# A two-layer hybrid backbone: first layer's down projection in two token passes, value products by column halves, branch weights ahead of logits

## What is computed

```python
h = modulate(rms_norm(x, norm1[l]), shift, scale)      # latent and context have their own vectors
z = h @ w_in[l]                                        # projections of four branches, gate logits
ys = [retention(z), gated_linear(z), grouped_attention(z), differential_attention(z)]   # each (T, 256)
m = sum(sigmoid(gate[i]) * (ys[i] @ w_branch[l, i]) for i in range(4))
x = x + g1 * (m @ w_out[l])
u = modulate(rms_norm(x, norm2[l]), shift2, scale2) @ w_up[l]
x = x + g2 * ((silu(depthwise_conv(u[..., :2816])) * u[..., 2816:]) @ w_down[l])
```

## Time and profile before

| what | us |
|---|---|
| median of 3 runs | 3206.71 |
| the profiled execution | 3203.14 |
| its span, first to last instruction | 3201.3 |
| TensorE matmuls busy | 2903.1 |
| GpSimd busy | 1420.2 |
| VectorE busy | 1322.9 |
| ScalarE busy | 597.4 |

### The profile page before, as it was taken

One profiled execution on the slowest core, in us unless ns is written; L12 is line 12 of the kernel. 1 busy time (PEld: TensorE's weight loads), 2 busy tenths in 40 slices (PEclk: granted clock), 3 DMA queues, 4 the chain that ended last, 5 costly groups with the idle time before them and its releaser, 6 DMA issues.

```text
span 3201.3 us, 38109 instructions
## 1 busy us (share of the span) xinstructions
PE 2903.1 (91%) x15848; PEld 2364.0 (74%) x15848; DVE 1322.9 (41%) x1730; ACT 597.4 (19%) x958; POOL 1420.2 (44%) x1357
## 2 busy tenths in 40 slices
PE   7899988989989788999999996997889896789999
PEld 7689977777868666888885655785667675668877
DVE  0622126643356754555551017315653576232231
ACT  1210032212124421100110003003211144011110
POOL 1233417722322353556540004453933333768886
PEclk6789979999989888999999997998999898899999
DMA  7331311221220451343442122221222104523322
GB/s 238 87 87 61 99 46 57 60 60 47 68 58 27 125 181 33 106 119 107 118 119 79 50 69 83 76 63 38 72 53 60 40 31 132 151 67 98 99 82 83
DMA packets 375480, 266.31 MB, mean 83 GB/s; under 512 B 9691, under 2 KB 348287, under 8 KB 374796
## 3 DMA queue, kind: packets, MB, share of 16 engines
q1 hardware_dynamic: 372928, 261.03, 27.8%
q10 hardware_dynamic: 1612, 2.75, 0.2%
q0 software_dynamic: 768, 0.09, 0.0%
HBM read 234.48 MB, written 29.36 MB: 82 GB/s over the span
## 4 chain that ended last, share of the span: by engine, by line
PE 79%; DVE 11%; POOL 4%; ACT 2%; DMA 2%; issue 1%; SPq 0%; DVEq 0%; ACTq 0%; POOLq 0%
PE ps L413 15%; PE ps L414 14%; PE ps L415 14%; PE ps L868 7%; PE ps L539 4%; PE ps L466 4%; PE ps L589 3%; PE ps L451 2%; PE ps L452 2%; PE ps L453 2%; PE ps L607 1%; PE ps L511 1%; POOL w_lo L991 1%; DMA ring<-in_w_branch 1%; DVE arena L1364 1%
## 5 line engine op out<-in xcount | busy, mean ns | idle before, releaser
L988 POOL TENSOR_TENSOR w_hi<-ring,tiny 128x512 fp32r<-128x512 f32 x524 | 582.2, 1111 | 1614.2 <-PE ps L415 744.6
L413 PE MATMUL ps<-hh,w_hi 128*128 128x512 f32 (+1 forms) x2272 | 844.8, 372 | 50.7 <-DVE hl L1355 50.7
L414 PE MATMUL ps<-hl,w_hi 128*128 128x512 f32 (+1 forms) x2272 | 818.9, 360 | 0.0
L415 PE MATMUL ps<-hh,w_lo 128*128 128x512 f32 (+1 forms) x2272 | 817.1, 360 | 0.0
L991 POOL TENSOR_TENSOR w_lo<-ring,w_hi 128x512 fp32r<-128x512 f32 x524 | 719.2, 1373 | 41.1
L413 PEld LDWEIGHTS ps<-hh,w_hi 128*128 128x128 f32 x2272 | 440.9, 194 | 157.9 <-issue 59.5
L415 PEld LDWEIGHTS ps<-hh,w_lo 128*128 128x128 f32 x2272 | 440.3, 194 | 64.6
L414 PEld LDWEIGHTS ps<-hl,w_hi 128*128 128x128 f32 x2272 | 442.0, 195 | 57.7 <-issue 1.0
L868 PE MATMUL ps<-arena,ring 128*128 128x512 f32 (+1 forms) x704 | 230.1, 490 | 1.2 <-DVE arena L1718 1.2
L868 PEld LDWEIGHTS ps<-arena,ring 128*128 128x128 f32 x704 | 134.6, 191 | 96.2 <-issue 85.8
L1648 DVE SCALAR_TENSOR_TENSOR xT<-ps,modv,xT 128x512 f32<-128x512 f32 (+1 forms) x48 | 30.3, 659 | 392.6 <-PE ps L868 197.6
(11 more groups left out here) (206 smaller groups left out, 3891.8 us busy)
## 6 DMA issues: line engine op xcount, KB each, us to landing
ring<-in_w_in SPq DMA_DIRECT2D x118, 512.0 KB, 4.1
ring<-in_w_mod SPq DMA_DIRECT2D x96, 512.0 KB, 3.9
ring<-in_w_up SPq DMA_DIRECT2D x88, 512.0 KB, 4.0
ring<-in_w_down SPq DMA_DIRECT2D x32, 512.0 KB, 4.1
logits<-arena SPq DMA_DIRECT2D x32, 384.0 KB, 2.4
arena<-logits SPq DMA_DIRECT2D x32, 384.0 KB, 3.4
ring<-in_w_branch SPq DMA_DIRECT2D x16, 512.0 KB, 4.9
ring<-in_w_out SPq DMA_DIRECT2D x16, 512.0 KB, 4.4
```

Of the source, the lines that this page charges most:

```text
L413: pe.matmul(acc, wh[:, k], hi[:, n, x:y], start=n == 0, stop=False)
L414: pe.matmul(acc, wh[:, k], lo[:, n, x:y], start=False, stop=False)
L415: mm = pe.matmul(acc, wl[:, k], hi[:, n, x:y], start=False, stop=n == whole - 1)
L988: pool.tensor_tensor(wh[:, 0:count], w, one[:].unsqueeze(2).to_broadcast([P, count, P]), ALU.mult).then_inc(*up("w_lead", ("lead", key, j)))
```

## The change

**First layer's down projection.** It is done in two passes over tokens. The latent pass (chunks `down`) is split as in the second layer, with `ffh` and `ffl` made in both layers. The context pass (new chunks `dctx`, the same weights loaded a second time, not split) multiplies plain fp32 over 256 columns. Accumulators are one bank per output tile, `u % 4`. VectorE adds to the residual per stream (`residual_of`) and squares at once; TensorE sums the squares per stream (`sum_of_squares`), the latent ones between the output tiles and in the context pass, and the next layer's norm 1 runs per stream (`norm_of`): the latent one beside the context pass. The first two projections of the second layer (queries, latent only) wait for the latent norm alone; the third waits for the context part. The store to `x_kept` in the second layer moves from the first to the fourth projection's chunk.

**Value products.** Two heads are multiplied together in all branches but gla: the values (128 keys x 64) are the stationary operand and the turned weights (128 keys x 128 queries) move; the first head's result goes to partitions 0 to 63, the second's to 64 to 127 of `("oT", l, b, t)`. ScalarE (ret, dif) or VectorE (gqa) copies it to `o_turned`, and two transposes (`turn_back`) bring it to the former layout. In the softmax branches the products of a pair stand behind the transposes of the head after it, and the turning back of tile t - 1 in head 1 of tile t. The last tile of ret and gqa is turned back behind the next branch's first projection.

**Order.** SP issues branch weights two chunks ahead of the logits of an output tile (`AHEAD`); the last logits are stored with the third `wb` chunk. One gate tile moves from dif to behind dif, and there it comes before `turn_outputs`.

```diff
-AMONG = {0: dict(ret=8, gla=10, gqa=7, dif=7), 1: dict(ret=8, gla=10, gqa=7, dif=7)}
+AMONG = {0: dict(ret=8, gla=10, gqa=7, dif=6), 1: dict(ret=8, gla=10, gqa=7, dif=6)}
...
+        order += [("dctx", l, n // 3, n % 3) for n in range(3 * KT) if W[l] > LAT]
...
-    return key[0] not in ("mod", "slice") and not (key[0] == "down" and W[key[1]] > LAT)
+    return key[0] not in ("mod", "slice", "dctx")
...
+        squares_of = {"lat": lambda k: sqb[1][:, k % 2, 0:LAT], "ctx": lambda k: arena[:, (8 + k) * T:(8 + k) * T + CTX]}
+        span_of = {"lat": (0, LAT), "ctx": (LAT, T)}
...
+        o_turned = prep_flat[:, 0:512].rearrange("p (b c t) -> p b c t", b=2, c=2)
...
+            def sum_of_squares(part, k):
+
+                key, (x, y) = ("norm", 1, part), span_of[part]
+                if k == 0:
+                    for s, n in room(key, 4 if part == "lat" else 5):
+                        pe.wait_ge(s, n)
+                pe.wait_ge(*at(("sq", 1, part, k)))
+                pe.matmul(psum(key)[:, 0:y - x], K["ones"], squares_of[part](k), start=k == 0, stop=k == KT - 1).then_inc(
+                    *up("pe_squares", ("squ", 1, part, k), *([("full", key)] if k == KT - 1 else [])))
...
-            def value_product(l, b, t, h, weights, *also):
-                pt = weights[:, h % 2].rearrange("p (m n) -> p m n", n=P)
-                hv = h // 2 if b == "gqa" else h
+            def value_products(l, b, t, first, weights, *also):
+
+                pt = [weights[:, s].rearrange("p (m n) -> p m n", n=P) for s in range(2)]
+                c = first // 2
                 for m in key_tiles(t):
-                    mm = pe.matmul(psum(("o", l, b, t))[:, 64 * h:64 * h + 64], pt[:, m],
-                                   v[:, hv // 2, m, 64 * (hv % 2):64 * (hv % 2) + 64], start=m == key_tiles(t)[0], stop=m == NT - 1)
-                mm.then_inc(*up("pe_values", ("pv", l, b, t, h), *([("full", ("o", l, b, t))] if h == 3 else []), *also))
+                    for s in range(2):
+                        vt = v[:, 0, m, 64 * c:64 * c + 64] if b == "gqa" else v[:, c, m, 64 * s:64 * s + 64]
+                        mm = pe.matmul(psum(("oT", l, b, t))[64 * s:64 * s + 64, P * c:P * c + P], vt, pt[s][:, m],
+                                       start=m == key_tiles(t)[0], stop=m == NT - 1)
+                mm.then_inc(*up("pe_values", ("pv", l, b, t, first), ("pv", l, b, t, first + 1),
+                                *([("full", ("oT", l, b, t))] if c else []), *also))
+
+            def turn_back(l, b, t, *also):
+
+                pe.wait_ge(*at(("free", ("oT", l, b, t))))
+                acc = psum(("o", l, b, t))
+                for c in range(2):
+                    mm = pe.transpose(acc[:, c * P:(c + 1) * P], o_turned[:, t % 2, c], ident)
+                mm.then_inc(*up("pe_values", ("full", ("o", l, b, t)), *also))
+
+            def last_turn_back(l, b):
+                t = NQ[l] - 1
+                for s, n in room(("o", l, b, t), 5):
+                    pe.wait_ge(s, n)
+                turn_back(l, b, t)
 
             def retention(l):
                 b = "ret"
...
@@ retention, TensorE @@
-                        value_product(l, b, t, h, pt_r)
+                    value_products(l, b, t, first, pt_r)
+                    if first == 0 and t > 0:
+                        for s, c in room(("o", l, b, t - 1), 5):
+                            pe.wait_ge(s, c)
...
@@ softmax, TensorE @@
-                    turn_weights(t, h, n >= 1)
-                    if n >= 1:
-                        base[("o", l, b, order[n - 1][0])] = 5 * 512 + 256
-                        value_product(l, b, *order[n - 1], pt_s, ("full", ("pt", l, b, t, h)))
+                    base[("oT", l, b, t)] = base[("o", l, b, t)] = 5 * 512 + 256
+                    if h % 2 == 0 and n > 0:
+                        turn_weights(t, h, True)
+                        value_products(l, b, *order[n - 2], pt_s, ("full", ("pt", l, b, t, h)))
+                    elif h == 1 and t > 0:
+                        turn_weights(t, h, True)
+                        turn_back(l, b, t - 1, ("full", ("pt", l, b, t, h)))
+                    else:
+                        turn_weights(t, h, False)
                 t, h = order[-1]
                 pe.wait_ge(*at(("free", ("pt", l, b, t, h))))
-                value_product(l, b, t, h, pt_s)
-                tenant[5] = ("o", l, b, t)
+                value_products(l, b, t, h - 1, pt_s)
...
@@ main loop, TensorE @@
+                            each = None
+                            if b == "ret" and j == 0:
+                                each = lambda k: ("hl", l, 1 if l == 0 else "lat", k)
+                            if b == "ret" and j == BR[b]["nq"] and l > 0:
+                                each = lambda k: ("hl", l, "ctx", k)
+                            projection(("f", l, b, j), hh, hl, W[l] if is_q(b, j) else T, banks(), each=each)
                             behind(("f", l, b, j))
...
+                        if j == 0 and BEFORE.get(b) in ("ret", "gqa"):
+                            last_turn_back(l, BEFORE[b])
...
+                last_turn_back(l, "dif")
+                among(l, "after", 0)
                 turn_outputs(l, "dif")
-                among(l, "after", 0)
...
-                    for s, n in room(acc_key, 2 * (u % 3), 2 * (u % 3) + 1):
+                    for s, n in room(acc_key, u % 4):
...
-                        if is_split(key):
+                        for j in range(2):
+                            pe.wait_ge(*at(("split", key, j)))
+                            mm = product(acc[:, 0:LAT], key, j, ffh, ffl, 0, LAT, count=min(4, count - 4 * j),
+                                         first=8 * c + 4 * j, whole=FT, each=(lambda k: ("ffl", l, k)) if u == 0 else None)
+                            mm.then_inc(*up("pe_half", ("half", key, j), *([("full", acc_key)] if 2 * c + j == 5 else [])))
+                    if l + 1 < DEPTH and u >= 2:
+                        sum_of_squares("lat", u - 2)
+                if l + 1 < DEPTH:
+                    for u in range(KT):
+                        acc_key = ("dctx", l, u)
+                        for s, n in room(acc_key, u % 4):
+                            pe.wait_ge(s, n)
+                        for c in range(3):
+                            key = ("dctx", l, u, c)
+                            next_chunk(key)
...
+                            for k in range(8 * c, min(8 * c + 8, FT)):
+                                mm = pe.matmul(psum(acc_key)[:, 0:CTX], raw(key)[:, k - 8 * c], ff[:, k, LAT:T],
+                                               start=k == 0, stop=k == FT - 1)
                             mm.then_inc(*up("pe_raw", ("used", key), *([("full", acc_key)] if c == 2 else [])))
+                        if u == 0:
+                            sum_of_squares("lat", KT - 2)
+                            sum_of_squares("lat", KT - 1)
+                    for k in range(KT):
+                        sum_of_squares("ctx", k)
...
@@ SP @@
+            AHEAD = 2
...
-                if n >= LATE and chunks[n - LATE][0] == "g" and key[0] != "wb":
+                if n >= LATE and chunks[n - LATE][0] == "g" and not (key[0] == "wb" and key[2] > AHEAD):
                     store_logits(chunks[n - LATE])
-                if key == ("wb", l, 0):
-                    for late in chunks[n - LATE:n]:
+                if key == ("wb", l, AHEAD):
+                    for late in chunks[n - LATE + 1:n - AHEAD]:
                         store_logits(late)
-                if key == ("mod", 0, MOD0 - 1) or key == ("f", 1, "ret", 0):
+                if key == ("mod", 0, MOD0 - 1) or key == ("f", 1, "ret", 3):
                     for k in range(KT):
-                        sp.wait_ge(*at(("free", ("x", k)) if l == 0 else ("free", ("down", 0, k))))
...
-                if key[0] == "wb":
-                    u = key[2]
+                if chunks[n - AHEAD][0] == "wb":
+                    u = chunks[n - AHEAD][2]
...
@@ ScalarE @@
+            def norm_of(part):
+
+                key, (x, y) = ("norm", 1, part), span_of[part]
+                act.wait_ge(*at(("full", key)))
+                act.activation(rs[:, x:y], psum(key)[:, 0:y - x], ACT.Sqrt, bias=eps).then_inc(*up("act_free", ("free", key)))
+                for k in range(KT):
+                    act.wait_ge(*at(("scaled", 1, part, k)))
+                    act.activation(hh[:, k, x:y], tb[:, k % 2, x:y], ACT.Identity,
+                                   bias=modv[:, k, int(x > 0):int(x > 0) + 1]).then_inc(*up("lead_ready", ("hh", 1, part, k)))
...
+            def outputs_out(l, b, t):
+
+                key = ("oT", l, b, t)
+                act.wait_ge(*at(("full", key)))
+                if t >= 2:
+                    act.wait_ge(*at(("full", ("o", l, b, t - 2))))
```

(50 more changed lines are left out.)

80 lines of the change are left out of this document (42 added, 38 removed).

## The result

| | median us | lowest to highest | runs | ratio to before, 95% interval |
|---|---|---|---|---|
| before, same chip | 3205.85 | | 4 | 1 |
| the change | 3104.11 | 3097.84 to 3112.55 | 4 | 0.9683 [0.9653, 0.9714] |
| predicted | 3109 | 3072 to 3166 | | |

A forecast was written before the change was run, and what follows sets the result against it. TensorE was taken to bound the kernel, busy 2903.1 of 3201.3 us. Steps of -28, -43, -18 and -8 sum to -97, so 3203.1 becomes 3106, and 3.6 for the median gives 3109 us; range 3072 to 3166.

The forecast's parts named there:

- B: Value products of two heads in column halves, turned back afterwards: -43 us, bounds -52 and +12.
- C: Branch merging, weights loaded ahead of logits: -18 us, bounds 0 and -28.
- A: First layer's down projection in two passes, with the norm behind it per stream: -28 us, bounds -38 and -12.
- D: One gate tile moved behind the last branch, filling TensorE's wait there: -8 us, bounds 0 to -14.
- The idle before the second tile: Latent down pass: TensorE idles 9.4 us, the second tile's first weights queued behind a modulation slice awaiting its ring slot.
- the row halves: Attention scores with neighbours in different row halves, 24 records in 1.53 us, taken as nearest price for value products.
- without overlap: Rival on value products: column halves don't work side by side, so no gain there; 3163 us, chance 0.19.
- swallowed: Rival: engines beside TensorE take the value products' gain in the attentions, only retention keeps it; 3142 us, chance 0.13.
- unhidden loads: Rival on value products: column halves undo hiding of weight loads, 0.228 us a record; 3307 us, chance 0.06.
- the stall behind the restored stream: Layer 0's merging: logits wait behind the 3 MB residual load; 6 us of the 12 us stall stay.
- crowding loads: Branch merging: loads at 206 GB/s, above the stage's 193, get in each other's way; 5 us back.

The follow-up runs named there:

- e6: The changed kernel with the last four modulation slices of the weights loaded three down chunks later; 3099.5 us, ratio 0.9679 to before.
- e4: The changed kernel with the moved gate tile put back inside differential attention and none behind it; 3111.03 us, ratio 0.9704 to before.
- e5: The changed kernel with all value products of a group's first head before the second's, so neighbours share a column half; 3146.56 us, ratio 0.9822 to before.
- e2: The changed kernel with value products as before, one head at a time and no turning back; 3148.1 us, ratio 0.9817 to before.

## Why the prediction was right, step by step

**Sum.** Predicted -97 on the profiled execution, measured -97.0; 3109 against 3104.11 us. The mechanisms are the ones that were named, but the match to the last microsecond is luck. The edited stages give 92 us, and 5.4 of those are the granted clock of one stretch; the rest comes from stages where the two kernels do the same. The repeated change is 95.9 us of medians under before, the first 101.7. Inside B and C errors cancel, as shown below. One sum doesn't come out: the bounds given for A, C and D reach from 3083 to 3151, not from 3080 to 3138.

**A, -28 predicted; -25.3 in the trace, 26 by undoing.** The idle before the second tile was to be 9.4 us and is 10.66, by the mechanism named, which e6 confirms. The latent pass was to end 154 us after zero and ends at 154.4. (The 113.76 us that the prediction quotes from the earlier trace rows stand in the earlier trace rows.) The context pass was to end at 239 and ends at 235.6 (1866.0): its sums start at once, and no last residual stands between. But the chain behind it was mis-sized, and it is why A gives 25 and not 28. I gave 13 us from there to the strips, a third of the joint norm, and had the strips at 252; they begin at 256.9, 21.3 us behind the context's sums. (My zero before, 1677.65, was the first down product; from the end of the up projection, 1676.4, the old strips stand at 281.7, so they came 24.8 us nearer.) VectorE and GpSimd in order of time:

```profile
1877.07 1.26 DVE L1433 SCALAR_TENSOR_TENSOR hl<-arena,modv,hh 128x256 fp32r<-128x256 f32 x1
1878.36 1.36 DVE L1440 SCALAR_TENSOR_TENSOR arena<-xT,tiny,arena 128x256 f32<-128x256 f32 x1
1879.65 0.47 DVE L1433 SCALAR_TENSOR_TENSOR hl<-arena,modv,hh 128x256 fp32r<-128x256 f32 x1
1880.16 0.48 DVE L1440 SCALAR_TENSOR_TENSOR arena<-xT,tiny,arena 128x256 f32<-128x256 f32 x1
...
1887.34 1.09 DVE L1542 SCALAR_TENSOR_TENSOR arena<-dist,arena 128x896 f32<-128x896 f32 x1 [3.53 <-ACT arena L1274]
```

```profile
1878.12 1.32 POOL L1054 TENSOR_TENSOR w_lo<-ring,w_hi 128x512 fp32r<-128x512 f32 x1
1889.46 1.04 POOL L1051 TENSOR_TENSOR w_hi<-ring,tiny 128x512 fp32r<-128x512 f32 x1 [10.02 <-PE ps L420]
```

Over 256 columns a scaling (L1440) takes 1.36 to 1.40 us and a rest (L1433) 1.26 while GpSimd splits weights, and either takes 0.48 from 1879.65 on, after GpSimd's last split ended. The eight tiles take 14 us, where a third of the old time gave 8. And the strips wait 3.53 us for ScalarE's exponentials. Before they waited 5.91, inside the 23.4 us of which I took a third: a cost that doesn't shrink with the columns. The Trainium skill (SBUF — State Buffer, Who interferes with whom) says that a VectorE operation with both inputs in SBUF contends with GpSimd's reads; these rows agree. A wait I had not seen at all is the 5.71 us of the third projection: ScalarE, which empties the first projections' banks, is in the context norm.

**B, -43 predicted; 43 by undoing (38 against the repeated change).** A group was to be 1.53 us by the row halves and is 1.46. The busy time falls by 70.9 us, of which 12.0 go into the turning back (8.5 predicted) and 7.6 into waits for exponentials; 51 are left. The cheaper group (3.6 us over 52) and the dearer turning back (3.5) cancel. The difference to 43 is inside the uncertainty of two ratios (13 us). What I took off differential attention by a guess of a third (6.7 us) is about the 7.6. The trace shows no gain of B and D in layer 1's last attention (-0.5 us): there D costs about what B gives, 118.2 us before, 126.5 with D alone, 118.6 with both, and 114.4 with B and not D (e4). I had counted D's loss of filler as waits alone; the granted clock is lower too, from 0.91 to 0.85 between before and D alone. TensorE's waits for exponentials grew by 10.3 us in both layers together, where over 10 in each would have spoken against me. The rivals on B: without overlap (3163) is what e5's kernel comes near to (3147), which doesn't alternate; of the gain only a sixth was swallowed (3142 needed three quarters); and unhidden loads (3307) would show records of 0.228, where even with neighbours in the same half a load and its stream fit in 0.100.
The Trainium skill (TensorEngine Tiling (Array Packing), Performance Considerations) names the swap of operands with twofold column tiling; the estimate from it was 1.35 us a group. The trace has 1.46, so the factor of two nearly holds.

**C, -18 predicted; -20.0 in the trace, 26 by undoing.** Layer 0's products take 84.2 us where 84 was worked out, and the stall behind the restored stream is 6.12 us on TensorE (6.68 on VectorE) where 6 was. In layer 1 I predicted no stall of its own; it has one of 7.58, and still C gave 9.2 there. The two mergings were to give 11 and 12 less 5 for crowding loads, and give 10.8 and 9.2. Layer 0 shows no crowding at all, and what layer 1 lacks has the cause just named, so -18 came near by two errors: a stall left out and a crowding put in. Undoing shows 6 us more than the trace's stages, within the uncertainty of its ratio.

**D, -8 predicted; 9 alone (0.9971 [0.9954, 0.9989]), 7 by undoing, within scatter.** The tile fills the wait at the turning as forecast (15.0 to 2.1 us). What it leaves behind was counted as 40% of 13.5 us for both layers; in the traces it is 8.8 us gained in layer 0's stage and 4.2 lost in layer 1's, a net of 5.

## What to carry to other kernels

Price a matmul by starts in a stretch, and take the nearest shape that does what the new one will: row halves gave column halves to within 5%. When a stage is cut into narrower pieces, don't scale a whole chain by the columns: fixed waits stay, and the other engines that now work beside it slow it. A stall that the sum names can be taken away before the change is made: both named here, the slice before the second tile's weights and the 3 MB load before the logits, were worth 11 us more in one comparison and 23 in the other. And filler that is moved out of a stage with waits can cost more than it fills: look at each layer's stage by itself, and at the clock there.

## What the hardware showed beyond expectation

**Column halves in fp32.** 64-column weights and 128 moving columns: 0.061 us a record where neighbours alternate between the halves, 0.100 in the same half. The 24 weight loads of a group take 1.29 us there (PEld, the line of the value products), 0.054 each, while 128-column loads took 0.115 each.

**The same instructions, up to 13 us apart.** Up to grouped attention in layer 0 the change and all its variants but e2 and e5 issue the same work, yet its first scores start anywhere from 684.9 us (e6) to 698.1 (e4); the change has 691.5, and 690.8 when repeated. Part of it is in layer 0's retention, from the first scores to gla's first product: 194.9 to 195.1 us in four kernels and 200.3 in the five others, with nothing between. The last part of that stretch, in the change and in e4 (columns as above):

```profile
388.90:423.80 34.90, 34.58 (x295) 34.29 (x293) 0.00 (x0) 4.02 (x6) 13.85 (x12) 0.99 0.29 77
390.30:430.60 40.30, 40.30 (x300) 39.99 (x298) 0.00 (x0) 3.84 (x5) 13.83 (x12) 0.86 0.28 74
```

TensorE does nearly the same work in both, with 0.3 us of idle in the one and none in the other, and had no idle in the 40 us ahead. In e4 the clock spends part of the window at the lower of its two levels (1.2 of 2.4 GHz), and the window is 5.4 us longer. What makes it fall in one kernel and not in the other was not found. So a difference of 5 us or less can't be read from one span, only from its own stage at an equal granted clock, or from repeated timed runs.
